# Modulation panels worked four at a time, one whole group per visit, in a hybrid decoder step

## Chip, cores and metric

The kernel runs on one core of a Trainium2 chip, in one launch. The metric is the device time of that launch in microseconds. TensorE is called PE here, VectorE DVE, ScalarE ACT, GpSimd POOL; SyncE (SP) only issues DMAs.

## What is computed

One inference step of a decoder layer for 256 prompt tokens and 8 sample tokens, 264 columns in all, model width 2048. Nine modulation vectors of width 2048 per condition (one for the prompt, eight for the samples) scale, shift and gate three sub-layers:

```
mod = silu(c) @ w_ada + b_ada                      # w_ada 2048 x 18432, 9 vectors
h = h + 1/2*gate1 * SwiGLU1(rmsnorm(h)*(1+scale1)+shift1)        # d_ff 5632
xm = rmsnorm(h)*(1+scale_m)+shift_m
proj = xm @ w_in            # q/k/v of a gated DeltaNet mixer, z, q/k/v of windowed attention, gates
h = h + gate_m * w_out(sigmoid(gA)*(oA @ w_proj_a) + sigmoid(gB)*(oB @ w_proj_b))
h = h + 1/2*gate2 * SwiGLU2(rmsnorm(h)*(1+scale2)+shift2)
y = rmsnorm_final(h)
```

All weights are float32 in HBM and are each read once.

## The kernel before

**Panels.** Weights are cut into panels of 128 x 2048 float32 (1024 KB; 704 KB for the down projections). All of them go through `raw`, a ring of four slots (`RAW = 4`), in one fixed order that SP issues with DMAs. `panel_loaded` of a slot tells of a landing; SP waits on `slot_done` of the slot before it loads into it again, so load number r needs whatever load r-4 brought to be used up.

**Projection panels.** A matmul of full precision is made of three: ACT copies the panel rounded into `whi` (`split_hi`, L851, instruction at L856), DVE writes the remainder into `wlo` (`split_lo`, L1298, instruction at L1302) and with that frees the slot (`slot_done`). `whi` and `wlo` have two buffers each, so the split of panel s waits in `split_hi` until PE has used panel s-2 (`panel_used`). PE does 32 matmuls of `whi` with the tokens' hi and lo parts (L2016, L2017) and then 16 of `wlo` (L2024), in `panel` (L2007), called by `full` (L2106). Results go through four accumulator banks.

**Modulation panels.** `w_ada` is 144 panels, four to a group. PE takes them straight out of the ring, with no split: `ada` (L2079) waits for the load and issues four matmuls over 32 columns each (L2091; the trace records two for each), the last of which frees the slot. When a group (or, for the groups in `WHOLE`, four groups, a unit) is complete, ACT copies the sums to `arow` (`copy_rows`, L871), PE transposes them (`fold`, L2095, L2001) and DVE adds the bias (`take_ada`, L1314). The panels of groups in `WHOLE` (8 to 23 and 32 to 35) are loaded by one DMA with four pieces (L682), others by a plain one (L671).

**Where they stand.** 144 modulation panels are spread over the whole kernel. Five stretches have a body, a tuple that `mixed(n, m)` (L127) makes: the numbers 0 to n-1 of projection panels, with m entries `None` for modulation panels, spread evenly, one at a time. SP loads a body in its order (`body_loads`, L708), PE works it in its order (`panels`, L2117). The five are the first feed-forward's halves (28 projection panels with 16, then 44 with 24), q/k/v (24 with 20), the output projection (16 with 8), and the first half of the second feed-forward (44 with 12): 80 modulation panels, 20 groups. `spot` gives a projection panel's place in the body, from which `split_hi` and `split_lo` know its slot. `closed_behind` gives the groups that end behind a projection panel, for ACT's `copy_rows` and DVE's `take_ada`. On ACT a feed-forward pair of panels goes: silu of the even one, split of the panel two ahead, `copy_rows`, then the copy of the hidden tile, split of the next, `copy_rows`.

Of the kernel before, what the change touches and what calls it, by code (L numbers as in the profile page):

```python
# [112 lines left out]
def seq(base, stride, i):  # L113

    return At(base + stride * i) if isinstance(i, int) else At(base, (stride, i))
# [6 lines left out]
FF_HALF = UP + FF_DOWN  # L122
ADA_FIRST = 2 * KD
PLAIN = (0, 1, 2, 3)


def mixed(n, m):  # L127

    body = [0]
    for x in range(1, n):  # L130
        body.append(x)
        if x < n - 1 and x * m // (n - 2) > (x - 1) * m // (n - 2):
            body.append(None)
    return tuple(body)


BLK = 4
NBLK = BLK * QT
FF1_PLANS = ((mixed(UP - NBLK, 16), 1),), ((mixed(UP, 24), 1),)
FF1_BEGIN = (NBLK, 8, 2), (0, 0, 0)  # L140
QKV_BODY = mixed(CT, 20)
OUT_BODY = mixed(KD, 8)
FF2_PLANS = ((mixed(UP, 12), 1),), ((PLAIN, UP_IT),)
G_FF1_HALF = 6
# [63 lines left out]
def count(body):  # L208

    return sum(x is not None for x in body)  # L210
# [8 lines left out]
def closed_behind(body, panel, g):  # L219

    x, m = -1, 0
    for k, entry in enumerate(body):
        if entry is None:
            m += 1
            if m % 4 == 0 and x == panel:
                yield g + m // 4 - 1, k
        else:
            x = entry
# [71 lines left out]
def build(nc, t):  # L300
    ctx = ExitStack()
    with ctx:
# [38 lines left out]
        body = cursor[0]  # L341
# [506 lines left out]
        def _(act):  # L848
# [79 lines left out]
            def ffn(n, o, s0, r0, a0, plan, g0, last, begin=(0, 0, 0)):  # L928
                for body, rounds, p, r, g in stretches(plan, begin):
                    per, raws = count(body), len(body)  # L930

                    def one_round(i):
                        for u in range(per // 2):
                            s = seq(s0 + p + 2 * u, per, i)
                            a = seq(a0 + p + 2 * u, per, i)
                            done(s)
                            act.activation(sg[:, u % 2, :], acc[:, a.slot(BANKS), 0:NT], ACT.Silu)\  # L937
                               .then_inc(acc_taken[a.slot(BANKS)], 1)
                            split_hi(s + 2, seq(r0 + r + spot(body, 2 * u + 2), raws, i))
                            for grp, k in closed_behind(body, 2 * u, g0 + g):  # L940
                                copy_rows(grp, At(r0 + r + k))

                            wait_taken(act, a + 1)
                            act.activation(uhi[:, tiles(p // 2 + u, i, per // 2), :], hf[:, u % 2:u % 2 + 1, :], ACT.Copy)\  # L944
                               .then_inc(hidden_hi, 1)
                            split_hi(s + 3, seq(r0 + r + spot(body, 2 * u + 3), raws, i))
                            for grp, k in closed_behind(body, 2 * u + 1, g0 + g):
                                copy_rows(grp, At(r0 + r + k))

                    if rounds == 1:  # L950
                        one_round(0)
                    else:
                        with act.Fori(0, rounds) as i:
                            one_round(i)
# [80 lines left out]
            for x in range(CT):  # L1035
                split_hi(At(S_QKV + x + 2), At(R_QKV + 4 + spot(QKV_BODY, x + 2)))
                for grp, k in closed_behind(QKV_BODY, x, G_QKV):
                    copy_rows(grp, At(R_QKV + 4 + k))
# [958 lines left out]
        def _(pe):  # L1997
# [81 lines left out]
            def ada(p, g, r):  # L2079

                pe.wait_ge(panel_loaded[r.slot(RAW)], (r.turn(RAW) + 1).val(16))
                begins = p == 0 and (not whole(g) or g % ATL == 0)
                if begins and g:

                    pe.wait_ge(ada_rows, units(g))
                for j in range(QT):
                    k = QT * (g % ATL) + p if whole(g) else QT * p + j  # L2090
                    last = mm(mp[QR * j:QR * (j + 1), 2, :], csl[:, k, :], raw[:, r.slot(RAW), j * AG:(j + 1) * AG],  # L2091
                              start=begins, stop=p == KD // QT - 1 and ends(g))
                last.then_inc(slot_done[r.slot(RAW)], 1)

            def fold(g):  # L2095

                if not ends(g):
                    return
                pe.wait_ge(ada_rows, units(g + 1))
                if g:  # L2100
                    pe.wait_ge(ada_taken, units(g))
                for c in range(ATL):
                    last = turn(mp[:, 3, c * P:(c + 1) * P], arow[:, c * P:(c + 1) * P])
                last.then_inc(ada_folded, 1)

            def full(s, shift, a, rows):  # L2106
                fresh(a)
                panel(s, shift, [(to(a), rows, True, True)])
# [8 lines left out]
            def panels(body, s0, r0, a0, g0, i, begun=None):  # L2117

                m, n, closed = 0, count(body), []
                for k, x in enumerate(body):  # L2120
                    if x is None:
                        ada(m % 4, g0 + m // 4, At(r0 + k))
                        m += 1
                        if m % 4 == 0:
                            closed.append(g0 + m // 4 - 1)
                        continue
                    if begun and x == 0:
                        begun()
                    elif not (begun and x == 1):
                        full(seq(s0 + x, n, i), seq(r0 + k, len(body), i), seq(a0 + x, n, i), xs)  # L2130
                    for g in closed:
                        fold(g)
                    closed = []
# [15 lines left out]
            def ffn(n, o, s0, r0, a0, plan, g0, begun=None, begin=(0, 0, 0)):  # L2149
                for body, rounds, p, r, g in stretches(plan, begin):  # L2150
                    if rounds == 1:
                        panels(body, s0 + p, r0 + r, a0 + p, g0 + g, 0, begun)
                    else:
                        with pe.Fori(0, rounds) as i:
                            panels(body, s0 + p, r0 + r, a0 + p, 0, i)
                pe.wait_ge(hidden_lo, (2 * n + o) * HALF + DOWN)
                sd, ad = s0 + UP, a0 + UP
                shift = r0 + plan_end(plan, begin) - sd

                def down(i):  # L2160
                    for q in range(4):
                        s, a = seq(sd + 2 * q, 8, i), seq(ad + q, 4, i)
                        fresh(a)
                        panel(s, shift, [(to(a), us[0:DOWN], True, False)])
                        if q == 0:
                            pe.wait_ge(hidden_lo, (2 * n + o + 1) * HALF)
                        panel(s + 1, shift, [(to(a), us[DOWN:HALF], False, True)])

                with pe.Fori(0, 4) as i:
                    down(i)  # L2170
                if o:
                    total_squares(sq, sacc, 3 if n else 1)
# [41 lines left out]
            for o in range(2):  # L2214
                ffn(0, o, S_FF1 + o * FF_HALF, R_FF1_SECOND if o else R_FF1, A_FF1 + o * A_FF_HALF,
                    FF1_PLANS[o], G_FIRST + o * G_FF1_HALF, None, FF1_BEGIN[o])
            panels(QKV_BODY, S_QKV, R_QKV + 4, A_QKV, G_QKV, 0,
                   walked(S_QKV, A_QKV, R_QKV, lambda k: N_FIRST + k + 2, G_N1))

# [80 lines left out]
            for g in range(NG):  # L2300
                n, hh = divmod(g, H // HG)
# [415 lines left out]
```

## Time and profile before

| | us |
|---|---|
| median of 3 runs | 2734.27 |
| lowest, highest | 2733.51, 2735.07 |
| the profiled execution, its own time | 2732.95 |
| its span, first to last instruction | 2731.1 |
| PE busy in it | 2657.4 |
| DVE busy | 1411.5 |
| ACT busy | 1053.2 |
| mean granted clock of TensorE | 0.991 |

The profile has a page (busy shares, the span in slices, DMA queues, the chain that ended last, the costliest groups) and views of the trace behind it: instructions in order of time, busy time by stretch, waits by who ended them, and DMA issues with the time to landing. A matmul's length in the timeline overlaps the next one's, so what PE spends on a piece of work is read from the start of one row to the start of the next.

### The profile page before, as it was taken

What the parts mean: (1) busy time and instruction counts of PE and PEld (TensorE: products, weight loads), DVE (VectorE), ACT (ScalarE), POOL (GpSimd) and SP (SyncE); (2) the same over time, 40 slices, a digit from 0 to 9 for tenths busy, and PEclk for the clock granted to TensorE, in tenths of its full rate; (3) what the DMA queues carried; (4) which work ended last, traced back from release to release, by engine and by line L of the source; (5) the groups of instructions that cost most, each with busy time, mean ns of one, the idle gap of its engine ahead of it and who ended that gap; (6) DMA issues with size and microseconds to landing.
All of it is one profiled execution on the core that took longest, in us unless ns stands there. A gap on an engine that the chain in (4) does not pass through costs nothing.

```text
span 2731.1 us, 49457 instructions
## 1 busy us (share of the span) xinstructions
PE 2657.4 (97%) x21449; PEld 2484.4 (91%) x21449; DVE 1411.5 (52%) x1811; ACT 1053.2 (39%) x1086; POOL 21.8 (1%) x49
## 2 busy tenths in 40 slices
PE   6999999999999899999999999999899999999998
PEld 3788999999999788899989999889799999999997
DVE  3554445444455666555557555375544455444455
ACT  3343333333334322644434444343433333333442
POOL 0000000000000000000010000000000000000000
PEclk9999999999999999999999999999999999999999
DMA  9987755667655787433277655766666655544453
GB/s 383 365 306 258 260 189 184 239 240 265 244 204 180 269 292 295 142 111 123 108 270 265 226 213 203 273 239 256 220 216 229 213 184 183 193 184 173 156 187 130
DMA packets 130575, 605.57 MB, mean 222 GB/s; under 512 B 10464, under 2 KB 10720, under 8 KB 84336
## 3 DMA queue, kind: packets, MB, share of 16 engines
q1 hardware_dynamic: 125584, 582.06, 59.4%
q0 software_dynamic: 4256, 20.59, 1.9%
q8 instruction: 129, 2.11, 0.3%
q10 hardware_dynamic: 576, 0.56, 0.1%
q14 instruction: 30, 0.25, 0.0%
HBM read 590.55 MB, written 12.62 MB: 221 GB/s over the span
## 4 chain that ended last, share of the span: by engine, by line
PE 90%; DVE 4%; ACT 3%; DMA 2%; issue 1%; SPq 0%; DVEq 0%; ACTq 0%
PE acc L2016 24%; PE acc L2017 23%; PE acc L2024 23%; PE mp L2091 4%; PE acc L2279 2%; PE acc L2285 2%; PE acc L2280 2%; ACT whi L856 1%; DMA raw<-in_ada 1%; PE mp L2001 1%; DVE wlo L1302 1%; PE acc L2184 1%; PE acc L2185 1%; PE acc L2191 1%; PE mp L2346 1%
## 5 line engine op out<-in xcount | busy, mean ns | idle before, releaser
L1302 DVE TENSOR_TENSOR wlo<-raw,whi 128x2048 fp32r<-128x2048 f32 (+2 forms) x429 | 893.5, 2083 | 776.6 <-ACT whi L856 776.2
L2016 PE MATMUL acc<-xhi,whi 128*128 128x264 f32 x3840 | 964.1, 288 | 5.7 <-ACT whi L856 5.2
L2017 PE MATMUL acc<-xlo,whi 128*128 128x264 f32 x3840 | 950.7, 285 | 0.0
L856 ACT ACTIVATE whi<-raw 128x2048 fp32r<-128x2048 f32 (+2 forms) x429 | 747.3, 1742 | 514.3 <-PE acc L2024 353.0
L2016 PEld LDWEIGHTS acc<-xhi,whi 128*128 128x128 f32 x3840 | 725.6, 189 | 85.5 <-issue 84.6
L2017 PEld LDWEIGHTS acc<-xlo,whi 128*128 128x128 f32 x3840 | 726.8, 189 | 0.1
L2024 PE MATMUL acc<-xhi,wlo 128*128 128x264 f32 x3840 | 502.5, 284 | 0.0
L2024 PEld LDWEIGHTS acc<-xhi,wlo 128*128 128x128 f32 x3840 | 478.4, 188 | 0.0
L2016 PE MATMUL acc<-uhi,whi 128*128 128x264 f32 x1408 | 348.2, 284 | 0.0
L2017 PE MATMUL acc<-ulo,whi 128*128 128x264 f32 x1408 | 348.0, 284 | 0.0
L2017 PEld LDWEIGHTS acc<-ulo,whi 128*128 128x128 f32 x1408 | 265.3, 188 | 0.0
L2016 PEld LDWEIGHTS acc<-uhi,whi 128*128 128x128 f32 x1408 | 264.7, 188 | 0.0
L2024 PE MATMUL acc<-uhi,wlo 128*128 128x264 f32 x1408 | 192.2, 284 | 0.0
L2024 PEld LDWEIGHTS acc<-uhi,wlo 128*128 128x128 f32 x1408 | 179.8, 188 | 0.0
L2091 PE MATMUL mp<-raw,csl 128*32 128x512 f32 x1152 | 157.3, 629 | 19.8 <-DMA raw<-in_ada 11.9
L944 ACT ACTIVATE uhi<-hf 128x264 fp32r<-128x264 f32 (+1 forms) x80 | 33.9, 424 | 361.4 <-DVE hf L1454 361.4
L937 ACT ACTIVATE sg<-acc 128x264 f32<-128x264 f32 x80 | 31.3, 392 | 274.0 <-PE acc L2024 272.1
L2279 PE MATMUL acc<-xhi,whi 128*128 128x264 f32 x512 | 133.0, 294 | 0.0
L2280 PE MATMUL acc<-xlo,whi 128*128 128x264 f32 x512 | 128.0, 285 | 0.0
L1454 DVE TENSOR_TENSOR hf<-sg,acc 128x264 f32<-128x264 f32 x80 | 34.4, 430 | 137.3 <-PE acc L2024 137.3
L2279 PEld LDWEIGHTS acc<-xhi,whi 128*128 128x128 f32 x512 | 96.6, 189 | 2.4 <-issue 2.4
L2280 PEld LDWEIGHTS acc<-xlo,whi 128*128 128x128 f32 x512 | 96.7, 189 | 0.0
(374 smaller groups left out, 2002.9 us busy)
## 6 DMA issues: line engine op xcount, KB each, us to landing
raw<-in_up SPq DMA_DIRECT2D x160, 1024.0 KB, 4.8
raw<-in_ada SPq DMA_DIRECT2D x144, 1024.0 KB, 7.4
raw<-in_down SPq DMA_DIRECT2D x128, 704.0 KB, 4.0
raw<-in_win SPq DMA_DIRECT2D x69, 1024.0 KB, 6.9
raw<-in_wgate SPq DMA_DIRECT2D x32, 1024.0 KB, 4.8
blk<-in_up SPq DMA_DIRECT2D x16, 1024.0 KB, 7.6
raw<-in_wout SPq DMA_DIRECT2D x16, 1024.0 KB, 6.5
raw<-in_wproj SPq DMA_DIRECT2D x24, 512.0 KB, 4.6
```

Of the source, the lines that this page charges most:

```text
L856: act.activation(whi[:, s.slot(SPLIT), 0:width], raw[:, r.slot(RAW), 0:width], ACT.Copy)\
L937: act.activation(sg[:, u % 2, :], acc[:, a.slot(BANKS), 0:NT], ACT.Silu)\
L944: act.activation(uhi[:, tiles(p // 2 + u, i, per // 2), :], hf[:, u % 2:u % 2 + 1, :], ACT.Copy)\
L1302: v.tensor_tensor(wlo[:, s.slot(SPLIT), 0:width], raw[:, r.slot(RAW), 0:width], whi[:, s.slot(SPLIT), 0:width].bitcast(F32), ALU.subtract)\
L1454: v.tensor_tensor(hf[:, u % 2, :], sg[:, u % 2, :], acc[:, up, 0:NT], ALU.mult)\
L2016: mm(dst, w, xh, start=starts and k == 0, stop=False)
L2017: mm(dst, w, xl, start=False, stop=False)
L2024: last = mm(dst, wlo[:, b, (tile + k) * P:(tile + k + 1) * P], xh, start=False, stop=ends and k == len(xs) - 1)
L2091: last = mm(mp[QR * j:QR * (j + 1), 2, :], csl[:, k, :], raw[:, r.slot(RAW), j * AG:(j + 1) * AG], start=begins, stop=p == KD // QT - 1 an ...
L2279: mm(to(a), w, xh, start=k == 0, stop=False)
L2280: mm(to(a), w, xl, start=False, stop=False)
L2285: last = mm(to(a), wlo[:, b, k * P:(k + 1) * P], xh, start=False, stop=k == KD - 1)
```

## The change

A body now has its `None` entries in runs of four, one group each, and both halves of the kernel read it in different ways. SP still loads it in its order. PE, and `closed_behind` for ACT and DVE, follow a new generator `worked`, which yields a run of `None` before the projection panel that stands ahead of it. So a projection panel is loaded, then the four modulation panels behind it; PE works the four first and the projection panel after them. The runs stand behind panels 7, 13, 20, 26 (first feed-forward, first half), 7, 14, 21, 28, 35, 42 (second half), 5, 9, 14, 18, 22 (q/k/v), 7, 14 (output projection) and 14, 28, 42 (second feed-forward) of the load order.

```
+AHEAD_RUN = 4
 def mixed(n, m):
-    body = [0]
+    body, runs = [0], m // AHEAD_RUN
     for x in range(1, n):
         body.append(x)
-        if x < n - 1 and x * m // (n - 2) > (x - 1) * m // (n - 2):
-            body.append(None)
+        if x < n - 1 and x * runs // (n - 2) > (x - 1) * runs // (n - 2):
+            body += [None] * AHEAD_RUN
     return tuple(body)
+
+def worked(body):
+
+    k = 0
+    while k < len(body):
+        after = k + 1
+        while after < len(body) and body[after] is None:
+            after += 1
+        yield from ((None, at) for at in range(k + 1, after))
+        yield body[k], k
+        k = after
...
 def closed_behind(body, panel, g):
     x, m = -1, 0
-    for k, entry in enumerate(body):
+    for entry, k in worked(body):
...
             def panels(body, s0, r0, a0, g0, i, begun=None):
                 m, n, closed = 0, count(body), []
-                for k, x in enumerate(body):
+                for x, k in worked(body):
```

SP's queue around the first run, before: projection panels 4 to 8 of the first feed-forward's body, each `in_ada` a single modulation panel, each row with the slot that it waits for.

```order
L671 DMA raw<-in_up 128x2048 [waits slot_done1]
L682 DMA raw<-in_ada 128x4x512 [waits slot_done2]
L671 DMA raw<-in_up 128x2048 [waits slot_done3]
L682 DMA raw<-in_ada 128x4x512 [waits slot_done0]
L671 DMA raw<-in_up 128x2048 [waits slot_done1]
L671 DMA raw<-in_up 128x2048 [waits slot_done2]
L682 DMA raw<-in_ada 128x4x512 [waits slot_done3]
L671 DMA raw<-in_up 128x2048 [waits slot_done0]
```

The same queue after the change: panels 6 and 7, a group of four, panels 8 and 9.

```order
L684 DMA raw<-in_up 128x2048 [waits slot_done2]
L684 DMA raw<-in_up 128x2048 [waits slot_done3]
L695 DMA raw<-in_ada 128x4x512 [waits slot_done0]
L695 DMA raw<-in_ada 128x4x512 [waits slot_done1]
L695 DMA raw<-in_ada 128x4x512 [waits slot_done2]
L695 DMA raw<-in_ada 128x4x512 [waits slot_done3]
L684 DMA raw<-in_up 128x2048 [waits slot_done0]
L684 DMA raw<-in_up 128x2048 [waits slot_done1]
```

Panel 7 and the fourth panel of the group now share slot 3, and panel 8 takes the slot of the group's first.

PE at the first modulation panel of that body, before: the end of a projection panel, the visit (four matmuls), the beginning of the next.

```order
L2017 MATMUL acc<-xlo,whi 128x264
L2024 MATMUL acc<-xhi,wlo 128x264 x16
L2091 MATMUL mp<-raw,csl 32x512 x4
L2016 MATMUL acc<-xhi,whi 128x264
L2017 MATMUL acc<-xlo,whi 128x264
```

PE at the first group after the change: the end of panel 6, the group, the beginning of panel 7.

```order
L2030 MATMUL acc<-xlo,whi 128x264
L2037 MATMUL acc<-xhi,wlo 128x264 x16
L2104 MATMUL mp<-raw,csl 32x512 x16
L2029 MATMUL acc<-xhi,whi 128x264
L2030 MATMUL acc<-xlo,whi 128x264
```

Four visits of four matmuls have become one of sixteen, in front of the projection panel that was loaded ahead of the group.

## Rows read from the trace of the kernel before

**Rows 1.** Page, busy shares (time, share, instructions) and chain by engine.
```profile
PE 2657.4 (97%) x21449; PEld 2484.4 (91%) x21449; DVE 1411.5 (52%) x1811; ACT 1053.2 (39%) x1086; POOL 21.8 (1%) x49
...
PE 90%; DVE 4%; ACT 3%; DMA 2%; issue 1%; SPq 0%; DVEq 0%; ACTq 0%
```

**Rows 2.** Windows of PE: stretch, length, busy (instructions), granted clock, DMA share, GB/s.
```profile
195.50:360.70 165.20, 165.20 (x1333) 1.00 0.71 254
...
939.00:1102.00 163.00, 163.00 (x1309) 1.00 0.80 284
```

**Rows 3.** Timeline of PE, feed-forward: start us, length us, engine, line, operation.
```profile
248.13 1.06 PE L2091 MATMUL mp<-raw,csl 128*32 128x512 f32 x8
...
253.13 2.10 PE L2024 MATMUL acc<-xhi,wlo 128*128 128x264 f32 x16
...
255.06 0.28 PE L2016 MATMUL acc<-xhi,whi 128*128 128x264 f32 x1
...
258.98 2.09 PE L2024 MATMUL acc<-xhi,wlo 128*128 128x264 f32 x16
...
261.00 1.07 PE L2091 MATMUL mp<-raw,csl 128*32 128x512 f32 x8
```

**Rows 4.** Timeline of PE, two modulation panels in one visit.
```profile
116.70 1.92 PE L2091 MATMUL mp<-raw,csl 128*32 128x512 f32 x16
118.56 0.39 PE L2184 MATMUL acc<-xhi,whi 128*128 128x264 f32 x1
```

**Rows 5.** Timelines of DVE and PE: remainders, and what PE begins when a panel ends.
```profile
257.99 2.29 DVE L1302 TENSOR_TENSOR wlo<-raw,whi 128x2048 fp32r<-128x2048 f32 x1 [1.30 <-ACT whi L856]
...
263.33 2.29 DVE L1302 TENSOR_TENSOR wlo<-raw,whi 128x2048 fp32r<-128x2048 f32 x1 [3.05 <-ACT whi L856]
...
1079.22 1.06 PE L2091 MATMUL mp<-raw,csl 128*32 128x512 f32 x8
...
1081.44 2.28 DVE L1302 TENSOR_TENSOR wlo<-raw,whi 128x2048 fp32r<-128x2048 f32 x1
...
1840.62 1.07 PE L2091 MATMUL mp<-raw,csl 128*32 128x512 f32 x8
...
1843.66 2.29 DVE L1302 TENSOR_TENSOR wlo<-raw,whi 128x2048 fp32r<-128x2048 f32 x1 [2.30 <-ACT whi L856]
```

**Rows 6.** DMA issues, 904:905, 925:926, 1044:1044.9, whole page: count, KB, us to landing.
```profile
raw<-in_ada SPq DMA_DIRECT2D x1, 1024.0 KB, 5.6
...
raw<-in_ada SPq DMA_DIRECT2D x1, 1024.0 KB, 6.1
...
raw<-in_ada SPq DMA_DIRECT2D x1, 1024.0 KB, 4.6
...
raw<-in_ada SPq DMA_DIRECT2D x144, 1024.0 KB, 7.4
```

**Rows 7.** Timeline of PE, [idle before]; then windows, columns as in rows 2.
```profile
32.67 0.71 PE L2113 MATMUL mp<-sacc,con 128*128 128x264 f32 x2 [1.85 <-DVE sacc L1437]
...
931.55 0.36 PE L2016 MATMUL acc<-xhi,whi 128*128 128x264 f32 x1 [1.79 <-ACT whi L856]
...
1124.00 0.59 PE L2228 MATMUL mp<-ghi,one_l 128*128 128x264 f32 x1 [3.42 <-DVE C L1629]
...
1942.65 0.36 PE L2016 MATMUL acc<-xhi,whi 128*128 128x264 f32 x1 [2.01 <-ACT whi L856]
...
931.55:937.04 5.49, 5.49 (x33) 0.69 1.00 407
...
940.07:944.07 4.00, 4.00 (x37) 1.00 0.68 183
...
34.30:41.00 6.70, 4.69 (x20) 0.50 1.03 411
...
1123.20:1129.90 6.70, 5.90 (x26) 0.50 0.25 75
...
1942.40:1945.70 3.30, 3.05 (x25) 1.00 0.00 0
```

## Prediction, made before the changed kernel ran

> **What bounds the kernel now.** I read the page's busy shares and chain first: TensorE is busy 97% of the span and carries 90% of the chain that ended last [rows 1]. Then I asked for busy time by stretch over the five places where modulation panels stand among projection panels (both halves of the first feed-forward, q/k/v, the output projection, the second feed-forward). Two are shown, the first feed-forward's first half and q/k/v [rows 2]: PE's busy time equals the stretch, 165.20 of 165.20 us and 163.00 of 163.00, at full clock; the other three read alike. So no load, ScalarE or VectorE is late there, and whatever PE saves or waits in these stretches goes straight into the end time. All 80 panels that the change moves stand in them: 16 + 24 in the first feed-forward, 20 in q/k/v, 8 in the output projection, 12 in the second feed-forward.
>
> **What a visit costs.** In the timeline of PE, from the modulation panel at 248.13 to the next at 261.00 are 12.87 us, with two projection panels in them; two wlo phases with no visit between them are 5.85 apart (253.13, 258.98) [rows 3]. So one visit costs 12.87 - 2 x 5.85 = **1.17 us**: 1.00 until the next panel begins, the rest in slightly stretched matmuls on both sides. Where the kernel already takes two modulation panels in one visit, the next projection starts 1.86 after the first (116.70, 118.56) [rows 4], so a further panel in the same visit costs **0.86**. Four visits of one cost 4.68, one visit of four 1.17 + 3 x 0.86 = 3.75. Saved: 0.93 in each of 20 groups, **-18.6 us**. The work is the same; nothing else gets shorter. Fold, row copy and sums stay one per group (or unit), each behind the projection panel that follows the group.
>
> **What the order of the ring costs.** Call `a` the projection panel that is now loaded ahead of a group M0..M3 but worked behind it. The ring has four slots, and M3 is the fourth load after `a`, so it goes into the slot of `a`. It can be issued only when VectorE has finished the `wlo` remainder of `a`. That split can't run early: ScalarE's `whi` of `a` waits until PE has used panel a-2. So M3 is issued only about a microsecond before PE comes to the group. M0, M1 and M2 go into the slots of a-3, a-2 and a-1, freed (by the same steps, at 5.85 a panel) some 18, 12 and 7 us ahead of the group, and are in time.
>
> How late M3 is, with T the end of a-1 on PE:
> - Slot of `a` free. Feed-forward, even panel: previous panel ends 261.00, `wlo` from 263.33 for 2.29, so 4.62 after the end of a-2; odd panel: 255.06 to 257.99 + 2.29, 5.22; q/k/v: 1079.22 to 1081.44 + 2.28, 4.50; output projection: 1840.62 to 1843.66 + 2.29, 5.33 [rows 3, 5]. With 5.85 for a-1 (and some 0.04 of SP) M3 is issued at T - 1.19, T - 0.6, T - 1.31, T - 0.5.
> - Load. A modulation panel of the whole groups comes in four pieces; issued with nothing much else in flight it took 5.6 and 6.1; one in one piece took 4.6 [rows 6]. Others in the trace take 7 or more, but behind another load. Nothing is directly ahead of M3, and the next load starts 2 us behind it. I take 6.0 and 4.7.
> - PE wants M3 at T + 3 x 0.86 = T + 2.58.
>
> The waits are then: 8 groups in front of an even feed-forward panel, 4.81 - 2.58 = 2.23 each, 17.8; 5 in front of an odd one (7 and 13 in the first half, 7, 21, 35 in the second), 2.8 each, 14.0; 3 in q/k/v of four pieces, 2.1 each, 6.3; the 2 later ones of one piece, 0.8 each, 1.6; 2 in the output projection, 1.6 each, 3.2. Sum **+42.9 us**. With 5.6 for all four-piece loads it is 6.4 less, with 6.6 as much above 6.0, 9.6 more. This bound can't go below nothing: a wait on a load gives no time back, and every term of it lies on a PE that has no slack.
>
> **What is next behind it.** The panel after `a` goes into M0's slot, issued about T + 1.1, and lands behind M3, some 2.6 later at the rate of a full queue (407 GB/s in the stretch at 931.55 [rows 7]), so near T + 7.5; `whi` takes 1.9, ready T + 9.5. PE ends `a` at about T + 4.8 + 1.0 + 5.9 = T + 11.7. Slack 2 us, so it is covered; ScalarE's row copy stands behind that split and is also in time for the fold. VectorE's hidden product or convolution waits behind the late `wlo` by a few us, but its accumulator bank is wanted two panels later. Cost nothing; were M3 to land past T + 7 the same panel would still be 2 us early, since PE moves with M3. Between groups the ring refills: four to fifteen projection panels of 5.85 against loads of some 2.6.
>
> **The clock.** A wait of PE can cost more than itself. In the trace the granted clock went to its lower level, 1.2 GHz, after PE had waited 1.79 (at 931.55), 1.85 (at 32.67) and 3.42 (at 1124.00), and not after 2.01 (at 1942.65) [rows 7]. The first half of a panel behind the wait at 931.55 took 5.49 in place of 4.00: 1.5 us. The 16 waits of 2.1 to 2.8 lie inside this list, those of 0.8 to 1.6 below it. I take two in three of the 16, 11 x 1.5 = **+16 us**; bounds are none and all 16, with up to 2 us each where the lower level lasts longer (6.70 us at 0.50 behind the 3.42 wait), 0 to 32.
>
> The rule that speaks here is in the Trainium skill, "TensorE: Matmul & The Clock Gate", section "HAM oscillation — how this bites in real kernels": a matmul loop that waits for a DMA in each round falls to the half clock in every single round. By it all 16 waits would drop the clock, and the term would be 24 and not 16, the time 2782; the wait of 2.01 without a fall speaks against "every". The same section's rule of thumb counts only gaps longer than any forecast here; by it the term is zero and the time 2758, and this trace's fall behind 1.79 speaks against that.
>
> **Sum.** -18.6 + 42.9 + 16 = +40 us against the profiled execution, 2732.95 us (2731.1 of span and 1.9 around it); the median of the runs shown is 1.3 above it, so I forecast 2734.3 + 40 = **2774 us**.
>
> **Rivals.**
> - *Waits, but the clock holds.* Same waits, no fall: +24, 2758 us; with 5.6 loads 2752. For it: the 2.01 us wait. Against: three of four waits of this size were followed by a fall.
> - *Longer waits and a fall nearly every time.* Four-piece loads at 6.6 and 32 for the clock: -18.6 + 52.5 + 32 = +66, 2800 us. For it: the median of all modulation loads in the page is 7.4 [rows 6], though those are mostly behind another load.
> - *The last load of the four is in time* (ends on the other side). Place: the fourth panel of each group. If it landed by T + 2.58, nothing would wait and only the saving would be left: 2734.3 - 18.6 = 2716 us. Break-even is a wait of 0.93, a landing by T + 3.5, which from T - 1.19 is a load of 4.7 us. One-piece loads do that, four-piece ones don't in any row. If the four-piece loads took 4.7 alone, the waits would sum to about 22 and the time would be 2738, no change. To be faster the split of `a` would have to end a microsecond or more earlier too, and nothing in the change does that.
> - *The change doesn't group the work.* The built order shows one visit of sixteen matmuls in place of four of four, and `a` loaded ahead of them; so this is out.
>
> **How the numbers follow.** Forecast with some falls (2762 to 2788): 0.60. Clock holds (2750 to 2762): 0.18. Longer (over 2788): 0.12. No change within 0.2% (5.5 us, about what a measurement of this kernel can tell from none): 0.05. Faster: 0.05. So faster 0.05, same 0.05, slower 0.90. The range leaves out the last two and the tail of the longer case: 2750 to 2799.
>
> **What would show it.** The page after: idle time before the modulation matmuls, released by the DMA raw<-in_ada, grown by some 43 us in 18 to 20 new waits, each in front of the fourth panel of a group, never the first three. The q/k/v waits in the last two groups under 1 us. Visits of 32 records, 3.6 us without the wait. Stretches of half clock in the middle of the feed-forwards, where there are none now, about eleven. No wait on whi behind a group. I am wrong on the mechanism if the first or second panel of a group waits (the ring is behind by more than the one slot) or none does; wrong on size if the four-piece loads take other than 6.0 when alone; wrong on the clock term if the half-clock stretches number under five or over sixteen.

## The result: slower, 2777.28 us

The changed kernel takes 2777.28 us (median of 4 runs, 2774.53 to 2779.56), the kernel before in the same comparison 2733.89 (2732.74 to 2735.07): a ratio of 1.0161, 95% interval 1.0149 to 1.0173. That is 43.4 us more. The forecast was 2774, with 2750 to 2799 as its range. The profiled execution has a span of 2772.7 us, 41.6 above the one of before.

The page of the changed kernel: busy shares, chain by engine, chain by line (its first part is PE by line, then who else stands in it).

```profile
PE 2656.5 (96%) x21449; PEld 2496.2 (90%) x21449; DVE 1411.0 (51%) x1811; ACT 1054.5 (38%) x1086; POOL 21.7 (1%) x49
...
PE 83%; DMA 6%; DVE 5%; ACT 4%; issue 1%; SPq 0%; DVEq 0%; ACTq 0%
PE acc L2029 22%; PE acc L2030 22%; PE acc L2037 21%; DMA raw<-in_ada 5%; ACT whi L869 3%; DVE wlo L1315 3%; PE mp L2104 2%; PE acc L2298 2%; PE acc L2293 2%; PE acc L2292 2%; PE mp L2014 1%; PE acc L2197 1%; PE acc L2198 1%; PE acc L2204 1%; PE mp L2359 1%
```

The chain by line before, for comparison:

```profile
PE acc L2016 24%; PE acc L2017 23%; PE acc L2024 23%; PE mp L2091 4%; PE acc L2279 2%; PE acc L2285 2%; PE acc L2280 2%; ACT whi L856 1%; DMA raw<-in_ada 1%; PE mp L2001 1%; DVE wlo L1302 1%; PE acc L2184 1%; PE acc L2185 1%; PE acc L2191 1%; PE mp L2346 1%
```

Beside [rows 1] PE's busy time is the same to 1 us, because two things nearly cancel in it: the saving of visits, and matmuls that take longer at the lower clock or behind a wait. Yet PE fell from 90% to 83% of the chain. What grew is one repeating link, each part of which had 1% before: the load of a modulation panel (DMA raw<-in_ada 5%), the `wlo` remainder that frees its slot (DVE 3%) and the `whi` ahead of that (ACT 3%).

PE's waits, first of before, then of after (us in total, times, longest):

```profile
PE mp L2091 <- DMA raw<-in_ada: 11.9, 8, 4.5
```

```profile
PE mp L2104 <- DMA raw<-in_ada: 55.5, 27, 4.5
```

That is 43.6 us of idle more on this one pair. Twenty of the 27 waits are new and sum to 45.7 us; the other seven stand outside the groups and have 9.8 in place of 11.9. Each of the 20 stands in front of the fourth panel of a group, none in front of the first three. The five stretches that hold the groups, of before and of after (stretch, length, PE busy, granted clock, DMA share, GB/s), from the first projection panel of each to the stage behind it:

```profile
177.38:360.78 183.40, 183.25 (x1476) 1.00 0.69 247
489.22:775.42 286.20, 286.20 (x2314) 1.00 0.68 247
913.11:1104.22 191.11, 189.32 (x1485) 0.98 0.80 285
1808.09:1913.94 105.85, 104.39 (x841) 1.00 0.68 251
1924.34:2202.73 278.39, 276.38 (x2229) 0.99 0.62 216
sum 1044.95, PE 1039.53; mean PE 207.91
```

```profile
177.39:373.00 195.61, 183.36 (x1476) 0.98 0.67 231
501.44:804.27 302.83, 287.69 (x2315) 0.98 0.67 232
941.87:1137.68 195.81, 186.51 (x1484) 0.97 0.76 279
1840.75:1948.57 107.82, 103.11 (x840) 1.00 0.67 252
1958.42:2244.43 286.01, 276.17 (x2229) 0.98 0.60 210
sum 1088.08, PE 1036.83; mean PE 207.37
```

Together they are 43.1 us longer, against 41.6 for the whole span, so the whole loss is here: 12.2 (4 groups), 16.6 (6), 4.7 (5), 2.0 (2) and 7.6 us (3). Per group that is 3.0, 2.8, 0.9, 1.0 and 2.5: small where loads are in one piece or the split of `a` is early, large in the feed-forwards, in the order of the forecast's waits. The granted clock reads 0.98 in the first feed-forward, where it was 1.00.

One group close up, the first of the first feed-forward. PE by time:

```profile
218.89 2.78 PE L2104 MATMUL mp<-raw,csl 128*32 128x512 f32 x24
224.78 1.06 PE L2104 MATMUL mp<-raw,csl 128*32 128x512 f32 x8 [3.11 <-DMA raw<-in_ada]
```

SP by time (start, length):

```profile
211.86 6.71 SPq L695 DMA_DIRECT2D raw<-in_ada  x2
220.02 6.22 SPq L684 DMA_DIRECT2D raw<-in_up  x4
```

The DMA issues in 211.8:212.2, in 218:218.5 and in 220:220.4, the last number the us to landing:

```profile
raw<-in_ada SPq DMA_DIRECT2D x1, 1024.0 KB, 5.4
...
raw<-in_ada SPq DMA_DIRECT2D x1, 1024.0 KB, 6.5
...
raw<-in_up SPq DMA_DIRECT2D x1, 1024.0 KB, 7.2
```

PE does three panels (24 records) from 218.89 and then waits 3.11 us. SP's first row spans two loads: the third panel's issue at 211.86 and the fourth's, which ends 6.71 later and takes 0.37, so it began at 218.20, 0.69 before the group. It lands 6.5 us later, at 224.74; PE goes on at 224.78. The third panel, issued alone, had taken 5.4. The projection panel behind the fourth was issued at 220.02.

### The profile page after: what moved, and what is told of

It is laid out like the page before. It is cut to its first block, busy times and chain, and to the rows that moved or that the text cites. A ratio compares the mean times of both kernels' runs of the same rounds, so it can differ in the third digit from the quotient of the medians.

```text
span 2772.7 us, 49457 instructions
## 1 busy us (share of the span) xinstructions
PE 2656.5 (96%) x21449; PEld 2496.2 (90%) x21449; DVE 1411.0 (51%) x1811; ACT 1054.5 (38%) x1086; POOL 21.7 (1%) x49
## 4 chain that ended last, share of the span: by engine, by line
PE 83%; DMA 6%; DVE 5%; ACT 4%; issue 1%; SPq 0%; DVEq 0%; ACTq 0%
PE acc L2029 22%; PE acc L2030 22%; PE acc L2037 21%; DMA raw<-in_ada 5%; ACT whi L869 3%; DVE wlo L1315 3%; PE mp L2104 2%; PE acc L2298 2%; PE acc L2293 2%; PE acc L2292 2%; PE mp L2014 1%; PE acc L2197 1%; PE acc L2198 1%; PE acc L2204 1%; PE mp L2359 1%
## 5 line engine op out<-in xcount | busy, mean ns | idle before, releaser
L2104 PE MATMUL mp<-raw,csl 128*32 128x512 f32 x1152 | 153.2, 642 | 63.5 <-DMA raw<-in_ada 55.5
L2104 PEld LDWEIGHTS mp<-raw,csl 128*32 128x32 f32 x1152 | 29.2, 112 | 137.2 <-DMA raw<-in_ada 87.0
```

## Experiments

Each is compared with the kernel before, run beside it: 2732.78 us for the first four, 2737.31 for the other four. The changed kernel's 2777.28 stands beside 2733.89, so experiments are set against it by their distances from the kernel before.

### The fourth panel made short

```
-                        load_ada(At(r0 + k), g0 + m // 4, m % 4)
+                        if m % 4 == 3:
+                            load(At(r0 + k), t["ada"][4 * (g0 + m // 4) + 3, :, 0:AG], AG)
+                        else:
+                            load_ada(At(r0 + k), g0 + m // 4, m % 4)
```

> The changed kernel, but the fourth panel of each of the 20 groups is loaded only in its first 512 of 2048 columns; PE still does all four matmuls, three of them on what the slot held before, so the modulation vectors aren't the reference's. Theory (the wait is the fourth load, which can't start before the slot of panel a is free): a load of a quarter the size, issued about 1.2 us before the group, lands within some 3 us, close to the 2.6 us at which PE wants it, so at most 0.5 us are left of each wait, none of the half-clock stretches in the mixed bodies, and only the saving of the grouped visits remains: -18.6 us against the kernel before plus up to 10 of rest, 2716 to 2726 us. Rival (the ring as a whole is behind, by bandwidth): 15 MB less of 606 changes little, waits stay near 2.5 us or move to another panel of the group, 2760 to 2777 us.

Measured: 2714.94 us, ratio 0.9936 (0.9919 to 0.9952), 17.8 us faster than before and 1 us below the 2716 to 2726 expected. This kernel leaves out the load of three quarters of each fourth panel. Windows of its profiled execution over the same five stretches (only the sum and the first two):

```profile
176.50:356.28 179.78, 179.63 (x1476) 1.00 0.65 235
484.72:765.41 280.69, 280.69 (x2314) 1.00 0.65 234
...
sum 1029.47, PE 1023.10; mean PE 204.62
```

The first two are 3.6 and 5.5 us shorter than before, 0.9 per group, with no idle time. All 20 visits but one (in the second feed-forward, 0.24 us of idle) run through in one go:

```profile
218.00 3.64 PE L2107 MATMUL mp<-raw,csl 128*32 128x512 f32 x32
```

So the saving of grouped visits is real, and the whole loss of the change hangs on when the fourth panel lands. Of the 18.5 us by which this execution's span (2712.6) is shorter, 15.5 lie in the five stretches (1044.95 less 1029.47) and 3.0 outside them, where nothing of the groups stands; so the close match with the forecast's 18.6 is in part chance, while the 0.9 per group is not. Bandwidth as such is out: the third panels and the projection panels are as they were.

### The next projection panel held back

```
                     else:
+                        if k and body[k - 1] is None:
+                            r = At(r0 + k - 1)
+                            sp.wait_ge(panel_loaded[r.slot(RAW)], (r.turn(RAW) + 1).val(16))
                         load(seq(r0 + k, len(body), i), w[i * n + (w0 + x)])
```

> The changed kernel, but SP waits until the fourth panel of a group has landed before it issues the next projection panel. In the changed kernel the four-piece fourth load takes 5.4 to 6.9 us, mostly 6.3 to 6.9, with the next load issued 1.8 to 2.5 us behind it, while the third load, alone, takes 5.4 to 5.7. Theory (the load behind stretches it): the fourth loads take 5.5, each of the 16 four-piece waits shrinks by some 0.8 us, -13 us, and fewer stretches of half clock; the next projection panel then lands 3 us later, about T + 9.3, with whi ready at T + 11.2, just when PE wants it: 2755 to 2766 us. Rival (the four-piece load has this length by itself): fourth loads stay at 6.4, and the later projection panel adds waits on whi of up to 1 us in each group: 2777 to 2795 us.

Measured: 2760.02 us, ratio 1.0098 (1.0081 to 1.0114): 27.2 us over the kernel before where the changed kernel is 43.4 over, so 16 us better. A wait added to SP's queue made it faster. PE at the first group:

```profile
224.94 1.93 PE L2107 MATMUL mp<-raw,csl 128*32 128x512 f32 x8 [2.35 <-DMA raw<-in_ada]
```

SP behind it:

```profile
224.92 2.35 SPq L684 DMA_DIRECT2D raw<-in_up  x4
```

The fourth load, among the issues in 218:219.9:

```profile
raw<-in_ada SPq DMA_DIRECT2D x1, 1024.0 KB, 5.8
```

Over the 16 four-piece groups the fourth load took 5.3 to 6.0 us, 5.5 in the mean; in the changed kernel it took 5.4 to 6.9, mean 6.4. So the load that SP issues 1.8 to 2.5 us behind it costs it 0.9 us in the mean, though not each time: three of the changed kernel's 16 took 5.4, 5.5 and 5.8 with that load behind them. What in the queue makes the difference isn't shown. The 20 waits sum to 32.4 us in place of 45.7, and 2 are followed by the lower clock in place of 6. The price that was expected for it is also there, but small: two groups wait 0.8 and 1.05 us on `whi` behind them.

### Modulation panels in one piece

```
-                        load_ada(At(r0 + k), g0 + m // 4, m % 4)
+                        load(At(r0 + k), t["ada"][4 * (g0 + m // 4) + m % 4])
```

> The changed kernel, but in the five bodies every modulation panel is loaded in one piece (128 rows of 8 KB) and not in four (2 KB each); same bytes, other columns, so the modulation vectors aren't the reference's. Theory (the wait is issue to landing of the fourth load): it takes 4.75 as the one-piece ones in q/k/v and the output projection do; waits of 0.9 (even), 1.5 (odd), 0.8 (q/k/v) and 1.6 (output projection), in all 22 to 26 us, no stretch of half clock from them: -18.6 + 24 = +5, 2736 to 2744 us. Rival (the landing isn't what counts, PE waits on the slot's turn or on SP's queue): no change from 2777.

Measured: 2742.14 us (2738.73 to 2746.24), ratio 1.0039 (1.0025 to 1.0053): inside what the theory gave, 9.4 us over the kernel before where the changed kernel is 43.4 over. PE's wait in its first group:

```profile
223.00 1.06 PE L2104 MATMUL mp<-raw,csl 128*32 128x512 f32 x8 [1.32 <-DMA raw<-in_ada]
```

The load, among the issues:

```profile
raw<-in_ada SPq DMA_DIRECT2D x1, 1024.0 KB, 4.8
```

The fourth loads take 4.7 to 5.0 (one 5.3); waits are 0.5 to 1.5 us, and no stretch of half clock is left behind a group. In the first group the fourth load is issued as in the changed kernel, 0.69 us ahead; only its landing moved, by 1.8 us, and the wait with it (3.11 to 1.32). With loads of this length a group of four worked ahead is near its break-even, as the forecast had it for 4.7 us.

### Runs of two

```
-AHEAD_RUN = 4
+AHEAD_RUN = 2
```

> The changed kernel with AHEAD_RUN = 2: modulation panels two at a time, 40 visits of two, each still worked ahead of the projection panel loaded in front of it. Theory: the second of a pair goes into the slot of panel a-2, free some 12 us earlier, so nothing waits, and a visit of two costs 2.03 in place of 2 x 1.17: saves 0.31 in 40 visits, -12.4 us, with no half clock: 2719 to 2725 us. Rival (grouping itself is what costs, by bursts of loads): slower than before, 2740 or more.

Measured: 2721.71 us, ratio 0.9956 (0.9939 to 0.9972), 11.1 faster than before. Nothing of the computation is left out. The first two of its stretches, and the sum of the five:

```profile
177.38:358.39 181.01, 180.86 (x1476) 1.00 0.70 250
486.83:769.52 282.69, 282.69 (x2314) 1.00 0.69 249
...
sum 1034.98, PE 1029.58; mean PE 205.92
```

Its waits of PE on modulation panels, all outside the groups:

```profile
PE mp L2104 <- DMA raw<-in_ada: 9.8, 7, 4.5
```

The 40 visits of two begin their successor 1.85 us after their start, each, as in [rows 4], with no wait. 286.20 less 282.69 is 3.5 us for 12 visits of two, 0.29 each, against the 0.31 expected. So not grouping but the group of four is what hurts.

### Runs of four in load order

```
 def worked(body):
-    k = 0
-    while k < len(body):
-        after = k + 1
-        while after < len(body) and body[after] is None:
-            after += 1
-        yield from ((None, at) for at in range(k + 1, after))
-        yield body[k], k
-        k = after
+    for k, x in enumerate(body):
+        yield x, k
```

> One part of the change alone: runs of four, but PE works the body in the order in which SP loads it, so the projection panel a behind a group is loaded behind it too (the generator that reads the runs first is left out). Theory (four slots can't hold four modulation panels and the next projection panel): the fourth modulation panel is now early, since its slot is that of a panel two before; but a goes into the slot of the group's first panel, issued about T + 1.1, landing T + 5.9, whi ready T + 7.9, wanted T + 3.6: a wait of 4.3 us on ACT's whi in front of each of 20 projection panels, 87 us, and half clock behind nearly each, 20 x 1.5 to 3: -18.6 + 87 + 30 to 60 = +98 to +128 against before, 2832 to 2862 us. So the loading ahead is worth some 70 us. Rival (the four-slot ring is short in either order by the same amount): waits of 2.5 as in the changed kernel, 2770 to 2785 us.

Measured: 2842.77 us, ratio 1.0392 (1.0369 to 1.0415), 105.5 us over before. PE at the first group:

```profile
227.53 2.76 PE L2098 MATMUL mp<-raw,csl 128*32 128x512 f32 x24
...
234.66 0.56 PE L2023 MATMUL acc<-xhi,whi 128*128 128x264 f32 x1 [4.38 <-ACT whi L863]
```

The ACT row that it waited for:

```profile
232.61 1.91 ACT L863 ACTIVATE whi<-raw 128x2048 fp32r<-128x2048 f32 x1 [11.31 <-DMA raw<-in_up]
```

PE's waits on it:

```profile
PE acc L2023 <- ACT whi L863: 93.1, 26, 4.4
```

The second stretch, and the sum of the five:

```profile
510.48:828.58 318.10, 291.92 (x2314) 0.95 0.63 223
...
sum 1150.32, PE 1057.97; mean PE 211.59
```

All 20 groups are followed by a wait of 4.26 to 4.44 us on `whi`, as expected (4.3), and all 20 by a stretch at the lower clock, seven of them of the longer kind, 6.83 us. So the change's second half, loading `a` ahead, is worth some 62 us to the runs of four (105.5 less 43.4); it turns a wait of 4.3 on the next projection panel into one of 0.6 to 3.1 on the fourth modulation panel. It can't remove it: four slots hold either four modulation panels, or three of them and `a`.

### Runs of two in load order

The same edit of the generator with AHEAD_RUN = 2.

> Runs of two, and PE in load order. Theory: two modulation panels leave two slots for projection panels; the panel behind a pair has the slot of the panel two before it, free early, so nothing waits and loading ahead brings nothing: the same time as with runs of two worked ahead, 2718 to 2724 us (2721.7 there). Rival (any run needs the panel behind it loaded ahead): waits on whi of 1 us or more at 40 places, 2735 us or more.

Measured: 2724.57 us, ratio 0.9959 (0.9947 to 0.9971), the same ratio as with runs of two worked ahead (0.9956), and half a us above the 2718 to 2724 expected, beside a kernel before that was 4.5 us slower than in that comparison. Its trace has three new waits on `whi` in q/k/v, 1.01, 0.52 and 1.19 us, where ahead there are none; that is below what the comparison resolves. At the other 37 visits nothing waits, so with pairs the order matters little.

### The changed kernel again, twice

> The changed kernel once more, for the clock term: its runs spread over 5 us where those of before spread over 2. Theory: the waits are the same in each execution and the spread is the number of falls to half clock behind them, some 1.5 us each; this execution's span less 2772.7 is then 1.5 us times the difference in half-clock stretches inside the five mixed stretches (six there). Rival (loads vary): waits differ by some us in sum and the number of falls doesn't follow the time.

> The changed kernel a third time, same question as the run before: span against the number of half-clock stretches and the sum of the waits.

One execution each: 2774.26 and 2786.20 us, spans 2772.4 and 2784.4. They are called the second and the third execution below. The sums of the five stretches, first of the one, then of the other:

```profile
sum 1083.60, PE 1029.62; mean PE 205.92
```

```profile
sum 1097.58, PE 1044.75; mean PE 208.95
```

| execution | waits on raw<-in_ada, all | stretches at half clock behind the groups' waits | their length, us | PE busy, five stretches | span |
|---|---|---|---|---|---|
| changed kernel | 55.5 | 6 | 23.9 | 1036.83 | 2772.7 |
| second execution | 60.3 | 4 | 17.1 | 1029.62 | 2772.4 |
| third execution | 57.0 | 10 | 44.4 | 1044.75 | 2784.4 |

The third and fourth columns count only the stretches behind the groups' waits; others stand at the start of the stages, in each execution. The third execution has 15.1 us more of PE busy time than the second for the same instructions, and 27.3 us more at half clock behind the groups (and some 5 at the start of q/k/v): about half of the time at the lower level is lost. That is the theory's mechanism, but not its number. By 1.5 us per fall the spans should have been 3 us below and 6 above 2772.7; they are 0.3 below and 11.7 above. The rival has a part too: the 20 waits of the groups sum to 45.7 us in the changed kernel's profile, 48.4 in the second execution and 47.0 in the third. And a third part is neither: the second execution's five stretches are 4.5 us shorter than the profile's (1083.60 against 1088.08), and the rest of the kernel, where the change does nothing, is 4.2 us longer. Over three executions the falls are the largest variation inside the five stretches.

## Why the prediction was right, step by step

- **The saving of visits** (-18.6). Held: 0.9 per group in the first feed-forward without the waits, against 0.93. The total, 17.8 between medians, has 3 us in it from outside the five stretches.
- **Which load waits, and from when.** Held to 0.1 us. Fourth loads were issued 1.19 (even), 0.69 (odd), 1.41 (q/k/v) and 0.48 us (output projection) ahead of the group; forecast 1.19, 0.6, 1.31 and 0.5. The first three were never waited for.
- **The load's length** (6.0 and 4.7). The step that was mis-sized. One-piece loads took 4.75 to 4.86. Four-piece ones took 6.4 in the mean, in a case that the prediction described rightly (nothing ahead, the next load 2 us behind) but gave no price. Held back, the fourth load takes 5.5, so 6.0 was wrong either way: too long for a load alone, too short for one with another behind it. By the prediction's own sign (other than 6.0 when alone) it was wrong on size. The trace of before could have told. Its four-piece loads that had at most the last 0.4 us of another ahead of them are of two kinds. Four had no load issued behind them for 4 us and more and took 5.4 to 6.1, the two of [rows 6] among them. Seven had the next load 0.42 us behind and took 6.2 to 7.5. One of the seven (SP's rows, the second of two loads; then the first row's time to landing):

```profile
1961.49 0.38 SPq L682 DMA_DIRECT2D raw<-in_ada  x1
1961.91 3.43 SPq L671 DMA_DIRECT2D raw<-in_up  x2
...
raw<-in_ada SPq DMA_DIRECT2D x1, 1024.0 KB, 6.7
```

- **The sum of the waits** (+42.9). From a group's start to the projection panel behind it the 20 groups take 124.48 us, and 71.85 in the kernel with the short fourth panel: 52.6 us. Of that 3.0 are matmuls at the lower clock inside four visits, which belong to the next term. So the late fourth panels cost 49.6, 7 more than forecast: 6 for the load's length (16 x 0.4), the rest small things. PE sat idle for 45.7 of it and lost 0.2 more per group in starting again.
- **The clock** (+16, 11 falls of 16). Sized too high for the profiled execution, which had 6. What is left of 41.6 - (52.6 - 18.6) is 7.6 us outside the visits; with the 3.0 inside, some 10 for 6 falls, 1.7 each (forecast 1.5). The 7.6 is a remainder, and holds whatever else differs. The other two executions had 4 and 10 falls; 4 is under the five at which the prediction called this term wrong.
- **Luck in the total.** The two misses offset: 7 too few for the waits, 6 too many for the clock. That +40 lies so close to the profile's +41.6 (+43.4 between the medians) is owed to that.
- **What is next behind it.** Held. No wait on `whi` behind a group. In the group that begins at 262.56 in the first feed-forward, ACT begins the next panel at 271.09, after 8.03 us of idle time, and is done at 273.01, some 2.4 us before PE ends `a` at about 275.4: slack as forecast (2 us). ACT by time:

```profile
271.09 1.92 ACT L869 ACTIVATE whi<-raw 128x2048 fp32r<-128x2048 f32 x1 [8.03 <-DMA raw<-in_up]
272.91 0.57 ACT L892 ACTIVATE arow<-mp 128x512 f32<-128x512 f32 x1
```

- **Rivals.** The clock holding (2758) is out for this kernel: falls stood behind groups in all three executions. The kernel with the held-back load comes near that number (2760) by other terms, shorter waits and two falls. The rival on the other side, the fourth load in time, was made real by the short load, at 2715 for the 2716 given; its middle case, 4.7 us loads at 2738, by the one-piece loads at 2742. The rule cited from the Trainium skill ("TensorE: Matmul & The Clock Gate", section "HAM oscillation — how this bites in real kernels"), a fall in every round that waits for a DMA, held for the waits of 4.3 us in the runs of four in load order, 20 of 20, where PE waited for `whi` and that for a load. For the 16 waits of 1.2 to 3.4 us on four-piece loads it was 4 to 10, differing between executions. The example in that section has waits longer than those forecast here, which the prediction's sentence on it left out. Its rule of thumb, by which the term was nothing, did not hold in any of the three.

## What to carry to other kernels

In a ring of n slots, the load n places behind a panel can only start when that panel is used up. Where panels are used up only just ahead of need, as here, a run of n loads with nothing between them has one late, whichever order the consumer takes; this was seen for n = 4 in both orders. Runs of half the ring gave some six tenths of the saving (11.1 of 17.8 us) and no wait. Runs of three, and a ring of five slots, were not tried. Before grouping visits, set their saving (0.93 us for four) beside the wait that the load without lead will cause: its issue-to-landing time (4.7 to 6.4 us) less its lead (0.5 to 1.4) and the work in front of it (2.6). And take that time from a load that has the same neighbours in the queue.

## What the runs showed of the hardware

- A 1024 KB load in four pieces of 2 KB rows took 5.5 us in the mean alone (5.3 to 6.0) and 6.4 with one other load issued 1.8 to 2.5 us behind it (5.4 to 6.9); the same bytes in rows of 8 KB took 4.8 with the same load behind. So a later load on the queue can delay an earlier one, and holding it back can be worth a wait.
- The length of a wait doesn't decide alone whether the clock falls. In the profile of the changed kernel a wait of 2.44 us (at 1048.38) was followed by the lower level and one of 3.12 (at 268.46) wasn't; the same place differs between executions. Over the three executions and the kernel with the held-back load, the falls behind groups stood behind waits of 2.0 to 3.4 us, and about half of the waits in that range had none (22 with a fall, 24 without). Granted clock behind the two waits named:

```profile
1049.00:1052.30 3.30, 3.30 (x17) 0.50 1.02 429
...
268.50:272.00 3.50, 3.50 (x28) 1.00 1.01 426
```

Behind the 20 waits of 4.3 us it fell each time.
